# Inverse square roots of three mixers as powers on GpSimd, in a two-layer fp32 model on one core

## The chip, the cores and the metric

One core of a Trainium2 chip runs the whole program once. The metric is device time in microseconds (us), taken as the median of several runs. The engines are PE (TensorE, matmuls), DVE (VectorE), ACT (ScalarE), POOL (GpSimd) and SP (SyncE, which only issues DMAs here). Each takes its own instructions strictly in the order of its program and waits on counting semaphores for the others. Everything is float32.

## The reference, cut to what matters

Two blocks run one after the other on 256 tokens of width 1024. The first has two layers, each with three mixers side by side: HGRN2 (a gated linear recurrence), retention, and RWKV-7. The second has two layers of feed-forward, short convolution or latent attention, and attention to a memory; the change leaves its operations alone. The inverse square roots that the change touches are these:

```
# rwkv7_mixer, per head of 64
kk = kk * lax.rsqrt(jnp.sum(kk * kk, axis=-1, keepdims=True) + 1e-12)
y  = head_groupnorm(o, ln_g, ln_b, RWKV_GN_EPS) + bonus
# hgrn2_mixer
o  = rmsnorm(o.transpose(0, 2, 1, 3), norm_g)
# retention_mixer
o  = head_groupnorm(..., gn_g, gn_b, RET_GN_EPS)
# head_groupnorm
return (of - mu) * lax.rsqrt(var + eps) * g + b
```

## The kernel before

Each layer of the first block is cut into four quarters of the heads (q = 0 to 3). For each mixer and each engine there is a Python generator that issues that mixer's instructions for the four quarters and yields between steps: `rwkv_pe`, `rwkv_dve`, `rwkv_act`, `rwkv_pool` (called R), `hgrn_*` (H), `retention_*` (B, with no part on GpSimd). `weave` runs them by a string of `ORDER` that is written for each layer and engine: "R4 H2 B" means four steps of RWKV, two of HGRN, one of retention. So the order of instructions on each engine is fixed in the text, and an instruction that waits holds back all that stands behind it on its engine. After the mixers come the branch products (also woven), the output product, and then the second block, whose stages "conv", "queries" and "attention" have orders of their own.

On PE most steps of H and B, and the first sixteen of R in a quarter, are projections: 4 matmuls of the code with 256 columns, which the profile shows as 8 instructions (each fp32 matmul is two), from weights that SP loads into a ring of five slots. They need nothing but weights and a free PSUM bank, and so they are what fills PE's time while the recurrences, which are chains through PE, DVE, ACT and DMA, work out their next operand.

One quarter of RWKV goes like this. PE makes the projections, and from `rw_k` DVE forms `kk` and its square (L1100). PE sums the squares over each head with a matrix of ones (L787, "kkn"), which leaves the sum in every row, so the tile `rw_sig` with the sums is 128x512. DVE adds 1e-12 (L1103, "kkv"), ACT takes the root (L958, "kks"), DVE takes the reciprocal (L1108) and multiplies (L1110, "kk"). Only then may ACT overwrite `rw_sig` with the sigmoid of the decay code (L971), DVE scans it (L1130 to L1146), ACT takes exponentials (L976 to L980), DVE forms the operands (L1149 to L1158, "ops"), and PE makes the scores (L815 and L830). The rest of the quarter is a blockwise inverse on DVE (L660 to L701), which goes through DRAM and back, the products L729 to L895, and the same again for the backward direction; L848 is PE's first product with the masked scores.

At the end of a quarter each mixer norms its output `o`: DVE makes a variance of 4 or 8 numbers per partition ("varn", L1242 in `center_dve`, or L1524), ACT takes its root ("std": L1039 for RWKV, L1429 for HGRN, L1680 for retention), DVE the reciprocal (L1245 or L1527) and scales `o` (L1247 or L1529), and PE transposes it (L1289).

The HGRN loop has eight levels per quarter. For each, DVE (L1498, L1499) and POOL (L1563, L1564) form logarithms, ACT takes their exponentials (L1411, L1414), DVE (L1503) and POOL (L1568, L1570) multiply, PE makes the product (L1349) and DVE masks it in (L1511). POOL also sets `rw_scored_a` and `rw_scored_k` to zero twice in a quarter (L1061, L1062) and issues two small loads (L1054).

Of the kernel before, what the change touches and what calls it, by code (L numbers as in the profile page):

```python
# [10 lines left out]
ALU = mybir.AluOpType  # L11
# [100 lines left out]
def constants():  # L112
# [30 lines left out]
    for d, (strict, within) in enumerate(((p < c, p <= c), (p > c, p >= c))):  # L143
# [25 lines left out]
    ("conv", "tensor"):  # L169
        "C M2 C12 M2 C M2 C M C M C M C M C M C M C M C M2 C M C M C M C M3 C2 M C4 M C3 M3 C2 M3 C2 M21 ",  # L170
    ("queries", "tensor"):
        "Q M3 Q12 M3 Q2 M Q10 M2 Q M2 Q M4 Q M7 Q2 ",
    ("attention", "tensor"):
# [15 lines left out]
    ("conv", "vector"):  # L189
        "C M2 C10 M6 C4 M4 C5 M12 C M2 C2 M C M2 C M C M7 ",  # L190
    ("queries", "vector"):
        "Q M2 Q M Q6 M Q2 M3 Q7 M Q2 M Q M2 Q M Q M2 ",
    ("attention", "vector"):
# [3073 lines left out]
```

## Time and profile before

| | us |
|---|---|
| median of 3 runs | 3313.67 |
| lowest and highest | 3300.82 and 3321.72 |
| the profiled execution's own time | 3318.57 |
| its span, first to last instruction | 3316.7 |
| PE busy | 3075.4 |
| DVE busy | 1694.8 |
| ACT busy | 690.5 |
| POOL busy | 251.7 |

The profile is of one execution. Its own time is 1.9 us above its span and 4.9 us above the median, so a difference worked out in the trace is taken from 3318.57 and then moved down by 4.9. The two layers of mixers with their branches fill the first 2074 us of the span. The granted TensorE clock is given as a share of 2.4 GHz; the other level is 1.2 GHz, so a share c over a stretch means that 2(1-c) of it ran at 1.2 GHz.

### The profile page before, as it was taken

The numbers are of one execution on the slowest core, as the hardware profiler recorded it, in microseconds if no ns is written. First come the engines' busy times: TensorE is split into PE (matmuls) and PEld (weight loads), VectorE is DVE, ScalarE is ACT, GpSimd is POOL, SyncE is SP. The second block draws the span as 40 slices with busy tenths as digits, with TensorE's granted clock in tenths as the row PEclk, the third lists the DMA queues.
The fourth block names the chain that finished last, engine by engine and source line by source line (L and its number), as shares of the span: only waits on it lengthen the run. The fifth ranks groups of instructions, "written<-read, shape, count | busy, mean of one in ns | idle before, by whom it ended". The sixth has DMA issues, their size and how long they took to land. (4 is left out here: it accounts for less than half of the span.)

```text
span 3316.7 us, 45305 instructions
## 1 busy us (share of the span) xinstructions
PE 3075.4 (93%) x18996; PEld 2539.6 (77%) x18996; DVE 1694.8 (51%) x3491; ACT 690.5 (21%) x1343; POOL 251.7 (8%) x326
## 2 busy tenths in 40 slices
PE   8989997989999989999798999899979979997999
PEld 7878886868886878788687878695849749855794
DVE  3456556355321563755546421575237657746475
ACT  2323322132111232423123110100111011013100
POOL 0202121021000020202002100000000000000000
PEclk9999998989999999999798999999989989997999
DMA  5323232324324423333132243454425434531343
GB/s 206 104 79 125 78 114 79 102 70 130 117 93 156 151 66 107 103 92 118 41 123 77 76 142 140 148 170 159 152 78 173 169 111 141 174 108 76 127 167 126
DMA packets 153754, 395.56 MB, mean 119 GB/s; under 512 B 90288, under 2 KB 106800, under 8 KB 109648
## 3 DMA queue, kind: packets, MB, share of 16 engines
q1 hardware_dynamic: 51376, 367.94, 32.1%
q10 hardware_dynamic: 100608, 19.93, 3.0%
q0 software_dynamic: 1568, 4.79, 0.4%
q8 instruction: 151, 2.47, 0.3%
q14 instruction: 51, 0.42, 0.0%
HBM read 380.04 MB, written 12.59 MB: 118 GB/s over the span
## 5 line engine op out<-in xcount | busy, mean ns | idle before, releaser
L416 PE MATMUL bank<-h_features,weight_ring 128*128 128x256 f32 x4256 | 991.4, 389 | 7.8 <-DVE y_features L1266 2.8
L416 PEld LDWEIGHTS bank<-h_features,weight_ring 128*128 128x128 f32 x4256 | 812.2, 194 | 129.6 <-issue 7.3
L433 PE MATMUL bank<-weight_ring,h_features 128*128 128x256 f32 (+2 forms) x896 | 199.8, 375 | 2.0 <-DVE h_features L508 2.0
L433 PEld LDWEIGHTS bank<-weight_ring,h_features 128*128 128x128 f32 x896 | 162.5, 190 | 25.2 <-DVE h_features L508 2.3
L1922 PE MATMUL bank<-h_features,weight_ring 128*128 128x128 f32 x1408 | 171.9, 275 | 5.4 <-DVE h_features L508 5.4
L1922 PEld LDWEIGHTS bank<-h_features,weight_ring 128*128 128x128 f32 x1408 | 164.3, 192 | 6.1 <-DVE h_features L508 6.1
L1991 ACT COPY mem_normed<-bank 128x128 f32<-128x128 f32 x88 | 23.3, 265 | 482.6 <-PE bank L1922 476.9
L1746 PE MATMUL bank<-y_features,weight_ring 128*128 128x256 f32 x512 | 117.0, 380 | 0.0
L1746 PEld LDWEIGHTS bank<-y_features,weight_ring 128*128 128x128 f32 x512 | 95.9, 190 | 13.1 <-issue 0.7
L2074 DVE TENSOR_TENSOR mem_normed<-mem_normed,bank 128x256 f32<-128x256 f32 x88 | 37.1, 421 | 132.1 <-PE bank L1922 132.1
L1349 PE MATMUL bank<-hg_qs,hg_ks 128*128 128x128 f32 x512 | 76.2, 295 | 26.2 <-POOL hg_ks L1570 14.9
L1349 PEld LDWEIGHTS bank<-hg_qs,hg_ks 128*128 128x128 f32 x512 | 67.4, 202 | 37.3 <-DVE hg_qs L1503 25.0
L1922 PE MATMUL bank<-h_features,y_features 128*128 128x128 f32 x704 | 93.0, 275 | 0.0
L1922 PE MATMUL bank<-y_rwkv_features,y_hgrn_features 128*128 128x128 f32 x704 | 93.0, 275 | 0.0
L1922 PE MATMUL bank<-y_rwkv_features,y_features 128*128 128x128 f32 x704 | 93.0, 275 | 0.0
L1922 PE MATMUL bank<-ff_silu,weight_ring 128*128 128x128 f32 x704 | 93.0, 275 | 0.0
L1922 PE MATMUL bank<-h_features,y_hgrn_features 128*128 128x128 f32 x704 | 93.0, 275 | 0.0
L1922 PEld LDWEIGHTS bank<-h_features,y_features 128*128 128x128 f32 x704 | 85.7, 192 | 0.0
L1922 PEld LDWEIGHTS bank<-ff_silu,weight_ring 128*128 128x128 f32 x704 | 85.7, 192 | 0.0
L1922 PEld LDWEIGHTS bank<-y_rwkv_features,y_hgrn_features 128*128 128x128 f32 x704 | 85.7, 192 | 0.0
L1922 PEld LDWEIGHTS bank<-y_rwkv_features,y_features 128*128 128x128 f32 x704 | 85.7, 192 | 0.0
L1922 PEld LDWEIGHTS bank<-h_features,y_hgrn_features 128*128 128x128 f32 x704 | 85.7, 192 | 0.0
(520 smaller groups left out, 5003.7 us busy)
## 6 DMA issues: line engine op xcount, KB each, us to landing
weight_ring<-in_w_in SPq DMA_DIRECT2D x146, 1024.0 KB, 5.0
weight_ring<-in_f00w SPq DMA_DIRECT2D x33, 1024.0 KB, 4.8
weight_ring<-in_f01w SPq DMA_DIRECT2D x33, 1024.0 KB, 4.9
weight_ring<-in_f10w SPq DMA_DIRECT2D x33, 1024.0 KB, 4.8
weight_ring<-in_f11w SPq DMA_DIRECT2D x33, 1024.0 KB, 4.8
weight_ring<-in_w_b SPq DMA_DIRECT2D x16, 1024.0 KB, 4.8
weight_ring<-in_w_out SPq DMA_DIRECT2D x16, 1024.0 KB, 4.9
weight_ring<-in_conv_in SPq DMA_DIRECT2D x10, 1024.0 KB, 4.9
```

What stands on the lines that cost most here:

```text
L416: m = e.matmul(bank[:, j, :], w[:, k, j * P:(j + 1) * P], x[:, k, :], start=k == 0, stop=k == kt - 1, skip_group_check=True)
L433: m = e.matmul(bank[:, t * n:(t + 1) * n], x[:, k, t * P:(t + 1) * P], w[:, k, :], start=k == 0, stop=k == kt - 1, skip_group_check=True)
L1349: m = e.matmul(bank[:, t, h, :], H.k_[:, h, t * P:(t + 1) * P], H.q_[:, h, i * P:(i + 1) * P], start=True, stop=True, skip_group_check=True)
L1746: m = e.matmul(bank[:, j, :], w[:, k, j * P:(j + 1) * P], y[:, c * KT + k, :], start=k == 0 and c == 0 and j == 0, stop=k == KT - 1 and c ...
L1922: m = e.matmul(out, left[:, k, :], right[:, k, :], start=k == 0, stop=k == 3, skip_group_check=True)
L1991: e.copy(g.F.outs[at % 2][:, 7, :], g.banks.get(f, "p", c, 0)[:, 2 * P:3 * P]).then_inc(*S.act.up("first", f, c))
L2074: e.tensor_tensor(z[:, 0:2, :], z[:, 7:8, :].to_broadcast([P, 2, P]), first[:, 0:2, :], ALU.add).then_inc(*dve.up("u2", f, c))
```

## The change

The three roots on ACT and the reciprocals on DVE that follow them become one instruction on POOL each, a power with the exponent -0.5 from a one-column tile. The DVE steps that took the reciprocal now wait for POOL. Retention gets a generator on POOL for it. All the order strings are written anew, those of the second block too.

```diff
-        e.wait_ge(*dve.at("kkv", l, q))
-        e.activation(R.sig, R.sig, ACT.Sqrt).then_inc(*act.up("kks", l, q))
...
+def inverse_root_pool(e, g, S, z, *name):
+    e.tensor_tensor(z, z, g.minus_half.to_broadcast(list(z.shape)), ALU.pow).then_inc(*S.pool.up(*name))
...  rwkv_pool, in the loop over the quarters
         e.memset(R.state, 0.0).then_inc(*S.pool.up("state", l, q))
+        yield
+        e.wait_ge(*S.dve.at("kkv", l, q))
+        inverse_root_pool(e, g, S, flat(R.sig), "kks", l, q)
         for d in range(2):
...          the two memsets of scored_a and scored_k
+        yield
+        e.wait_ge(*S.dve.at("varn", l, q))
+        inverse_root_pool(e, g, S, R.var, "std", l, q)
...  rwkv_dve
-        e.wait_ge(*act.at("kks", l, q))
-        e.reciprocal(R.sig, R.sig).then_inc(*dve.up())
-        e.wait_ge(*dve.now())
+        e.wait_ge(*S.pool.at("kks", l, q))
         e.tensor_tensor(R.kk, R.kk, R.sig, ALU.mult).then_inc(*dve.up("kk", l, q))
...  center_dve, and in the same way hgrn_dve with H.ss
-    e.wait_ge(*S.act.at("std", *Q))
-    e.reciprocal(var, var).then_inc(*dve.up())
-    e.wait_ge(*dve.now())
+    e.wait_ge(*S.pool.at("std", *Q))
...  hgrn_pool, after the eight levels of a quarter
+        yield
+        e.wait_ge(*dve.at("varn", l, q))
+        inverse_root_pool(e, g, S, H.ss, "std", l, q)
...
+def retention_pool(e, g, l):
+    S, B = g.rt, g.B
+    for q in range(4):
+        yield
+        e.wait_ge(*S.dve.at("varn", l, q))
+        inverse_root_pool(e, g, S, B.var, "std", l, q)
+    yield
...  the start of two of the order strings
     ("mixers0", "tensor"):
-        "H2 R20 H2 R5 H11 R4 H R2 H6 B4 R2 B3 H B2 R B R5 H2 R2 B R B R H2 R2 B2 R4 B R4 H2 B R2 B R H2 R B R2 B "
+        "H2 R20 H2 R5 H7 R6 H11 R2 B5 R H R5 B R2 H2 R B R B2 R2 H2 R4 B R4 H2 B R2 B R H2 R B2 R2 B R6 H2 B4 H2 "
...
     ("mixers0", "gpsimd"):
-        "H R3 H10 R H6 R2 H16 R H10 R2 H6 R H9 R2 H7 R ",
+        "H B R4 H10 R H7 B R4 H16 R H B H4 R H R H2 R2 H8 B H2 R H5 R H R B H R2 H10 R2 ",
```

Read out step by step, the PE strings put this many projection steps (4 matmuls with 256 columns each) between the step with "kkn" and the first scores, L815, by quarter: layer 0: 11, 9, 4 and 10 before, 7, 8, 9 and 9 after; layer 1: 12, 9, 4 and 10 before, 10, 8, 4 and 9 after. The four steps with the code products stand there in both. In the DVE string of the first quarter of layer 0 two steps of H (L1451 to L1456) stand between L1133 and L1140 before, and none after. Between "kkv" and "kk" the DVE strings have no step of another mixer in the first quarter before or after; in the other quarters none to three, such as L1503.

In the POOL strings the power of "kks" stands right behind the loads and the memset of the state, before any HGRN level, in the first two quarters of layer 0 and the first of layer 1; in the second of layer 1 it stands behind the first level. In the third and fourth quarters it stands between the logarithms and the products of an HGRN level, or between two levels, and the power of RWKV's "std" of the quarter before stands one to three steps ahead of it, also inside the levels.

## Rows read from the trace of the kernel before

**Rows 1.** The page: busy time of each engine.
```profile
PE 3075.4 (93%) x18996; PEld 2539.6 (77%) x18996; DVE 1694.8 (51%) x3491; ACT 690.5 (21%) x1343; POOL 251.7 (8%) x326

```

**Rows 2.** Stretches: length, busy PE, PEld, DVE, ACT, POOL; granted clock, DMA share, GB/s.
```profile
0.00:2074.00 2074.00, 1915.42 (x12064) 1629.29 (x12064) 981.05 (x1927) 534.61 (x923) 248.69 (x320) 0.96 0.33 108
...
160.00:210.00 50.00, 37.19 (x213) 31.18 (x213) 42.81 (x79) 18.83 (x31) 11.25 (x13) 0.90 0.24 67
520.00:580.00 60.00, 38.29 (x167) 31.09 (x167) 49.01 (x88) 20.57 (x32) 9.16 (x12) 0.77 0.20 55
1560.00:1620.00 60.00, 40.15 (x167) 32.45 (x166) 48.45 (x87) 20.85 (x33) 9.16 (x12) 0.72 0.21 56
```

**Rows 3.** PE's waits up to 2120: for whom, us in total, times, longest.
```profile
PE bank L848 <- DVE rw_scored_k L1163: 31.2, 7, 6.7
...
PE bank L1349 <- POOL hg_ks L1570: 14.9, 5, 4.9
...
PE bank L815 <- DVE rw_a L1158: 7.4, 4, 2.0
```

**Rows 4.** The first quarter of layer 0 around "kks", in order of time.
```profile
61.12 0.68 DVE L1103 TENSOR_SCALAR rw_sig<-bank 128x512 f32<-128x512 f32 x1
...
65.89 0.69 DVE L1110 TENSOR_TENSOR rw_kk<-rw_kk,rw_sig 128x512 f32<-128x512 f32 x1
66.66 1.28 ACT L971 ACT_TABLE_LOAD   x1 [4.19 <-DVE rw_kk L1110]
...
72.84 0.17 DVE L1133 COPY rw_tot<-rw_bm 128x4 f32<-128x4 f32 x1
...
77.55 0.16 DVE L1140 TENSOR_SCALAR rw_mid<-rw_tot 128x4 f32<-128x4 f32 x1
...
82.46 0.69 DVE L1158 TENSOR_TENSOR rw_a<-rw_a,rw_bm 128x512 f32<-128x512 f32 x1
...
86.77 2.10 PE L815 MATMUL bank<-rw_kr,rw_a 64*128 64x256 f32 x16
```

**Rows 5.** From the chain that ended last: one projection step of PE.
```profile
2365.70 1.73 PE bank L416 x8
```

**Rows 6.** DVE's reciprocal of 128x512, and the two kinds of POOL product.
```profile
L1108 DVE RECIPROCAL rw_sig<-rw_sig 128x512 f32<-128x512 f32 x8 | 26.8, 3350 | 4.0 <-ACT rw_sig L958 4.0
...
L1568 POOL TENSOR_TENSOR hg_ks<-hg_ks,hg_kf 128x256 f32<-128x256 f32 x64 | 53.4, 835 | 177.5 <-ACT hg_ks L1414 177.5
L1563 POOL TENSOR_TENSOR hg_ks<-hg_bf 128x256 f32<-128x256 f32 x56 | 38.7, 691 | 301.2 <-PE bank L1349 301.2
```

**Rows 7.** The third quarter of layer 0 at "kks", in order of time.
```profile
525.05 1.00 DVE L1503 TENSOR_TENSOR hg_qs<-hg_qs,hg_q 128x512 f32<-128x512 f32 x1
...
525.47 1.18 POOL L1570 TENSOR_TENSOR hg_ks<-hg_ks,hg_kb 128x256 f32<-128x256 f32 x1
...
526.68 3.35 DVE L1108 RECIPROCAL rw_sig<-rw_sig 128x512 f32<-128x512 f32 x1 [0.62 <-ACT rw_sig L958]
...
530.07 0.69 DVE L1110 TENSOR_TENSOR rw_kk<-rw_kk,rw_sig 128x512 f32<-128x512 f32 x1
...
562.61 0.18 DVE L1245 RECIPROCAL rt_var<-rt_var 128x4 f32<-128x4 f32 x1 [2.79 <-ACT rt_var L1680]
```

**Rows 8.** PE at the end of the first quarter of layer 0.
```profile
202.57 1.11 PE L1289 MATMUL bank<-float_constants,hg_bf 128*128 128x128 f32 x4 [2.87 <-DVE hg_bf L1529]
```

**Rows 9.** ACT's table loads for the roots, by line.
```profile
L958 ACT ACT_TABLE_LOAD x8 | 10.3, 1283 | 0.1
...
L1429 ACT ACT_TABLE_LOAD x6 | 7.7, 1283 | 9.4 <-DVE rw_scored_k L1163 9.3
L1039 ACT ACT_TABLE_LOAD x6 | 7.7, 1283 | 0.1
...
L1680 ACT ACT_TABLE_LOAD x4 | 5.1, 1283 | 0.1
```

More of the change, by code:

```diff
@@ L149 @@
     ("mixers0", "tensor"):
[19 rows of a table removed]
[19 rows of a table added]
     ("conv", "tensor"):
-        "C M2 C12 M2 C M2 C M C M C M C M C M C M C M C M2 C M C M C M C M3 C2 M C4 M C3 M3 C2 M3 C2 M21 ",
+        "C M2 C12 M2 C M2 C M C M2 C M C M C3 M2 C M2 C M C2 M2 C2 M3 C2 M C4 M C3 M3 C2 M3 C M21 ",
     ("queries", "tensor"):
-        "Q M3 Q12 M3 Q2 M Q10 M2 Q M2 Q M4 Q M7 Q2 ",
+        "Q M3 Q12 M3 Q2 M Q6 M Q5 M3 Q M4 Q M7 Q2 ",
     ("attention", "tensor"):
[1 row of a table removed]
[1 row of a table added]
     ("mixers0", "vector"):
[13 rows of a table removed]
[15 rows of a table added]
     ("conv", "vector"):
-        "C M2 C10 M6 C4 M4 C5 M12 C M2 C2 M C M2 C M C M7 ",
+        "C M2 C10 M6 C4 M3 C5 M12 C M C M2 C2 M C M2 C M8 ",
     ("queries", "vector"):
-        "Q M2 Q M Q6 M Q2 M3 Q7 M Q2 M Q M2 Q M Q M2 ",
+        "Q M2 Q M Q6 M Q2 M3 Q6 M Q3 M Q M2 Q M Q M2 ",
     ("attention", "vector"):
[1 row of a table removed]
[1 row of a table added]
     ("mixers0", "scalar"):
[13 rows of a table removed]
[12 rows of a table added]
     ("conv", "scalar"):
@@ L213 @@
     ("attention", "scalar"):
-        "M X Y Z X M Y Z X2 M2 Y2 Z2 X M Y M2 Z X M X2 Y Z M2 X Y2 M Z2 M Y Z M X2 Y2 Z2 X M Y M2 Z X M X Y Z M2 "
-        "Y M Z M5 ",
+        "M X Y Z X M Y Z X2 M2 Z2 Y2 X M X M2 Y X2 Z M Y Z Y2 X M3 Z2 Y X2 M Z X M Y2 Z2 Y X M Z X Y M2 Y M Z2 M8 ",
     ("mixers0", "gpsimd"):
-        "H R3 H10 R H6 R2 H16 R H10 R2 H6 R H9 R2 H7 R ",
+        "H B R4 H10 R H7 B R4 H16 R H B H4 R H R H2 R2 H8 B H2 R H5 R H R B H R2 H10 R2 ",
     ("mixers1", "gpsimd"):
-        "R H R2 H10 R H6 R2 H16 R H10 R2 H6 R H9 R2 H7 R ",
+        "R H B R3 H12 R H5 B R2 H2 R2 H15 R B H7 R H R H R2 H7 B H R H5 R H R B H R2 H10 R2 ",
     ("mixers0", "sync"):
-        "H R4 H4 B6 H5 R4 B6 H5 B5 R4 B2 H2 B H B H B H B2 R4 B7 H4 B H B H B H B H B R8 ",
+        "H R4 H4 B6 H5 R4 B6 H5 B3 R4 B4 H2 B H B H B H B2 R4 B7 H3 B H B H2 B H B R7 H B R ",
     ("mixers1", "sync"):
-        "R4 H5 B6 H5 R4 B6 H5 B5 R4 B2 H2 B H B H B H B2 R4 B7 H4 B H B H B H B H B R8 ",
+        "R4 H5 B6 H5 R4 B6 H5 B5 R4 B2 H2 B H B H B H B2 R4 B7 H3 B H B H2 B2 H B R7 H R ",
     ("conv", "sync"):
@@ L955, in rwkv_act @@
             g.banks.empty(act, "vt", l, q, t)
-        yield
-        e.wait_ge(*dve.at("kkv", l, q))
-        e.activation(R.sig, R.sig, ACT.Sqrt).then_inc(*act.up("kks", l, q))
         for d in range(2):
@@ L1037, in rwkv_act @@
                     yield
-        e.wait_ge(*dve.at("varn", l, q))
-        e.activation(R.var, R.var, ACT.Sqrt).then_inc(*act.up("std", l, q))
-        yield
+def inverse_root_pool(e, g, S, z, *name):
+    e.tensor_tensor(z, z, g.minus_half.to_broadcast(list(z.shape)), ALU.pow).then_inc(*S.pool.up(*name))
 def rwkv_pool(e, g, l):
@@ L1427, in hgrn_act @@
         yield
-        e.wait_ge(*dve.at("varn", l, q))
-        e.activation(H.ss, H.ss, ACT.Sqrt).then_inc(*act.up("std", l, q))
-        yield
 def hgrn_dve(e, g, l):
@@ L1525, in hgrn_dve @@
         yield
-        e.wait_ge(*act.at("std", l, q))
-        e.reciprocal(H.ss, H.ss).then_inc(*dve.up())
-        e.wait_ge(*dve.now())
+        e.wait_ge(*S.pool.at("std", l, q))
         e.tensor_tensor(o3, o3, H.ss.unsqueeze(2).to_broadcast([P, 4, P]), ALU.mult).then_inc(
@@ L1678, in retention_act @@
             yield
-        e.wait_ge(*dve.at("varn", l, q))
-        e.activation(B.var, B.var, ACT.Sqrt).then_inc(*act.up("std", l, q))
-        yield
 def retention_dve(e, g, l):
@@ L3000, in clear_scratch_pool @@
     e.memset(g.nm_one, 1.0).then_inc(*g.st.pool.up("one"))
+    e.memset(g.minus_half, -0.5).then_inc(*g.st.pool.up())
     e.memset(zeros, 0.0).then_inc(*g.st.pool.up())
@@ L3011, in gpsimd_program @@
     for l in range(DEPTH):
-        weave(g, f"mixers{l}", "gpsimd", {"R": rwkv_pool(e, g, l), "H": hgrn_pool(e, g, l)})
+        weave(g, f"mixers{l}", "gpsimd", {"R": rwkv_pool(e, g, l), "H": hgrn_pool(e, g, l),
+                                          "B": retention_pool(e, g, l)})
     for S in (g.rw, g.hg, g.rt):
@@ L3075, in __init__ @@
         self.nm_ss, self.nm_one = sb("norm_sum", TT)[:, :], sb("norm_one", 1)[:, :]
+        self.minus_half = sb("minus_half", 1)[:, :]
         self.pos_i = sb("positions", TT, I32)[:, :]
```

87 rows, old and new, of the table ORDER are left out of this document.

## The prediction, made before the change was run

> **What bounds the kernel now.** I read the page's busy times first: PE is busy for 3075 us of 3317 and no other engine comes near it [rows 1]. So work that is taken from ACT or DVE is worth nothing by itself; it is worth what PE no longer waits. Next the stretches: the mixers take the first 2074 us, with PE busy for 1915, so 159 us are idle there. The idle time is not spread evenly. In 520 to 580, and in the same place of the next layer, 1560 to 1620, PE is busy for 38.3 and 40.2 of 60 us at a granted clock of 0.77 and 0.72, while DVE is busy for 49.0 and 48.5; 160 to 210 is the third such place [rows 2]. There DVE sets the pace. Then I read PE's waits by releaser: the largest, 31.2 us, is for the masked scores L1163 behind DVE's blockwise inverse, which the change doesn't touch; 14.9 us is for POOL's HGRN product; 7.4 us in four waits is for the operands L1158, whose chain begins at the root of "kks" [rows 3].
>
> **Part 1, the root of 128x512 ("kks"), 8 times.** Now: the sum with 1e-12 ends at 61.12 + 0.68 = 61.80 and the multiplication L1110 starts at 65.89, so root, reciprocal and hand-overs take 4.1 us; behind L1110 ACT loads a table for 1.28 us before the sigmoid L971 [rows 4]. The new order has one POOL instruction there, X us long. No row shows a power on POOL. From below: POOL's product L1563, 691 ns for 256 numbers per partition, or L1568, 835 ns, gives 1.4 to 1.7 us for 512 [rows 6]. From above: DVE's iterative RECIPROCAL of 512 takes 3.35 us [rows 6]; POOL's product takes 1.67 us for 512 against 0.69 for DVE's L1110 [rows 4, 6], so a function like the reciprocal at POOL's rate would be 3.35 x 2.4 = 8 us, and a power made of a logarithm, a product and an exponential as some ten passes over the data, each like a product of POOL, 15 us or more. I take 1.7 us, because the instruction is POOL's TENSOR_TENSOR with another operation and the rows nearest to it are POOL's TENSOR_TENSOR rows; the range keeps 1.4 to 15. The step is then 4.1 - 1.7 = 2.4 us shorter, and 1.3 us more where the sigmoid's table is still in, which it now can be, for no root comes between: 3.7 us of chain, 8 times.
>
> How long may X be before PE waits? In the first quarter the operands are ready at 82.46 + 0.69 = 83.15, and PE comes to L815 at 86.77 [rows 4]. The new string takes 4 of the 11 projection steps away from between; a step is 1.73 us [rows 5], so PE comes at about 79.9, or some 3 us earlier if its clock is full. The operands come earlier by 4.1 - X, by the table's 1.3 and by the 4.5 us between L1133 and L1140 (72.84 + 0.17 to 77.55), where H stood and doesn't now [rows 4]: at 73.3 + X. So X has room up to 3.5 to 6.5 us here; I take 5 for all quarters. Over both layers the strings take 5 projection steps net (8.7 us) out of this gap and put them in front of other waits.
>
> What PE gets back, by place:
> - 520 to 580, twice: DVE is the pace. L1503 came straight behind L1103 at 525.05, so L1110 could start at 525.05 + 1.7 = 526.8 in place of 530.07: 3.2 us. The root of retention makes DVE wait 2.79 us at 562.61, and a power of 4 numbers with its hand-over takes perhaps 0.3: 2.5 us [rows 7]. Together 5.7, twice: 11.4 us. A part of the 1.2 GHz time goes with it: 2 x 0.23 x 60 = 28 us of the first of these stretches ran at 1.2 GHz [rows 2], where busy PE loses half. I take 3 us for both.
> - The end of the first quarter, twice: PE waits 2.87 us for HGRN's normed output at 202.57 [rows 8]. The step is shorter by a table load of 1.28 us, and the new PE string has five steps of B in front of it: 2 x 2.9 = 5.7 us.
> - Two of the four waits of L815 for L1158 [rows 3] follow a "kks": 3.5 us.
> - The 5 steps set free, in front of the waits of L848 and L1349: of 8.7 us I count 3, since the planner of the order can't place them everywhere.
> Sum: 11.4 + 3 + 5.7 + 3.5 + 3 = 27 us.
>
> **Part 2, the 24 small roots.** Eight for each mixer, of 4 or 8 numbers per partition. A root, a reciprocal (0.18 us at 562.61) and where needed a table load of 1.28 us go; a POOL instruction on so few numbers comes. The gains on PE's path are in the list above. The rest is hidden: 8 + 6 + 6 + 4 = 24 loads for roots, 30.8 us of ACT [rows 9], on an engine that is busy for a fifth of the span. DVE loses 26.8 us of long reciprocals and some 4 us of short ones out of 981 in the mixers [rows 2, 6].
>
> **Part 3, POOL's queue.** POOL's own time is free (249 us busy of 2074 [rows 2]). But POOL now waits inside its order for "varn" and "kkv", and behind that stand the next HGRN logarithms and products, for which PE waits already (14.9 us in 5 waits [rows 3]). In third and fourth quarters such a wait stands between the logarithms and the product of a level. In the first quarter only the memsets of the scores stand behind it, due more than 10 us later. I count nothing for this in the forecast, and price it below.
>
> **Part 4, the other strings** (conv, queries, attention) move a few steps and no work; nothing, within 3 us either way.
>
> **A shared path between DVE and POOL.** L1503, a DVE product with both operands in SBUF, took 1.00 us at 525.05 while POOL ran, and POOL's L1570, which then overlapped it, took 1.18 us at 525.47 [rows 7] against 0.69 for DVE's product of the same shape L1110 and 835 ns for POOL's products [rows 4, 6]. One held the other up. The Trainium skill, page "SBUF — State Buffer", section "SBUF: two separate sides", says that the shared ports of the two are locked for a whole instruction and that a DVE operation with two SBUF inputs then waits it out; the trace agrees, with these two rows. By that rule a long power would also hold the L1503 that some new DVE strings put between "kkv" and "kk", but L1110 waits behind it anyway: it adds one product, 0.7 us, in those quarters.
>
> **The rivals.**
> Rival 1, the power is slow. It decides from X = 5 us on: DVE stands at L1110 and every other mixer's DVE step behind it too, so each further us is one us of PE in each of 8 quarters, and a quarter more for the lower clock. The gain of 27 is used up at X = 5 + 27/10 = 7.7 us. At X = 12 the price is 7 x 8 x 1.25 = 70 us, of the gain about 20 stay: +50, so 3369 by the profiled execution's count and 3364 as a median. For it: a power is no simple operation, and even DVE takes 6.5 ns per number for a reciprocal, five times its product. Against it: the fastest rows of that kind on POOL. The Trainium skill, page "GPSIMD Engine Reference", section "Elementwise — side-by-side cycle accounting", says that bodies of three or more operations run at roughly 3 operations a cycle at 1.2 GHz; if a power were 40 operations, an estimate by that page is 13.3 x 512 / 1.2 GHz = 5.7 us, and with 80 operations 11 us. No row here shows it.
> Rival 2, POOL's queue eats the gain. Four waits a layer (the "kkv" and RWKV's "varn" in the inner quarters) stand inside HGRN levels; if each holds PE's L1349 by 2.5 us, half of the longest such wait now (4.9 [rows 3]), that is 20 us: -7 in all, 3311 by the profiled count, 3307 as a median.
> Rival 3, it doesn't do what it says: ACT goes on loading tables, because exponential, sigmoid and logarithm alternate, so the 1.28 us behind L1110 stays. That costs 8 x 1.3 = 10 us of chain and at most 5 us of PE: inside rival 2's range.
>
> **How the numbers follow.** The forecast: 3318.6 - 27 = 3291.6 by the profiled execution's count, 4.9 lower as a median: 3287. Chance 0.48, its own range 3262 to 3305. Rivals 2 and 3 with no measurable change, a power between 5 and 9 us among them: 0.24, 3300 to 3325. Rival 1: 0.28, from 3340 up; at X = 15 the price is 10 x 8 x 1.25 = 100, less 20: 3394. The range leaves out the upper half of rival 1 and a little below: 3258 to 3375. One per cent is 33 us, about what a measurement of this kernel can tell from no change. The forecast passes that bound in 4 cases of 10, 0.20 in all; rival 1 gives 0.28 slower; the rest, 0.52, is within one per cent.
>
> **What would show it.** In the profile after: one POOL TENSOR_TENSOR on `rw_sig` x8; near 1.7 us the forecast holds, over 5 rival 1. L1110 starts some 2 us behind the end of L1103. No table loads for roots in the mixers, and ACT's loads fewer by 24 or more. DVE's wait at 562 gone, PE busier than 38 us in what was 520 to 580. Rival 2 would show as more than 15 us of waits of L1349 for POOL, with POOL idle before its powers. What would make all of it wrong: the new order leaving PE without projections at a place that was full before.

## The result, and the profile after

The changed kernel takes 3942.64 us (median of 4 runs, 3934.4 to 3948.25) against 3317.69 us for the kernel before in the same session: a ratio of 1.1905, 95% interval 1.187 to 1.1939. It is 625 us slower. The forecast was 3287 us with a range up to 3375, so it was wrong by far, and outside the range.

First the page of the kernel after: the span, the busy time of each engine, and in the slices the rows of PE, POOL and PE's granted clock.

```profile
span 3940.1 us, 45238 instructions
...
PE 3087.7 (78%) x18996; PEld 2547.8 (65%) x18996; DVE 1662.1 (42%) x3459; ACT 633.8 (16%) x1275; POOL 946.7 (24%) x359
...
PE   6497489288199947856963973998998998998899
...
POOL 4523612811910063164156037000000000000000
PEclk9698799689699978977986996999998999998799
```

PE does the same work as before, 3087.7 us against 3075.4 [rows 1], in a span 623.4 us longer: it stands idle for 852 us where it was idle for 241. POOL is busy for 695 us more. In the slices PE is at 2 and 1 tenths where POOL is at 8 and 9, and at 3 to 6 where POOL is at 4 to 7, where a power is split over two slices. The chain that ended last, by engine, and the groups of the new instruction (the name of the group, then busy us and mean ns, then the idle time of POOL ahead of it):

```profile
PE 66%; POOL 17%; DVE 10%; DMA 4%; issue 1%; ACT 1%; ACTq 0%; DVEq 0%; SPq 0%
...
L1037 POOL TENSOR_TENSOR rw_sig<-rw_sig,minus_half 128x512 f32<-128x512 f32 x8 | 657.5, 82187 | 233.8 <-DVE rw_sig L1106 233.7
```

One power of 512 numbers per partition takes 82.2 us. The forecast took 1.7 us, from the rows of POOL's products [rows 6]. The small ones, from the groups of POOL:

```profile
L1037 POOL TENSOR_TENSOR rw_var<-rw_var,minus_half 128x8 f32<-128x8 f32 x8 | 14.6, 1827 | 275.2 <-DVE rw_var L1243 275.2
...
L1037 POOL TENSOR_TENSOR hg_ss<-hg_ss,minus_half 128x4 f32<-128x4 f32 x8 | 8.4, 1056 | 106.5 <-DVE hg_ss L1520 106.5
```

(1827 - 1056) / 4 = 193 ns for each number by these two, (82187 - 1827) / 504 = 159 ns from 8 to 512. So the small powers of this kernel alone would have said some 99 us for 512 numbers (193 ns x 512, an estimate).

Who waits for it. PE's waits (for whom, us in total, times, longest), which answer to [rows 3]:

```profile
PE bank L1348 <- POOL hg_ks L1564: 394.4, 8, 78.8
PE bank L815 <- DVE rw_a L1159: 85.9, 5, 78.4
PE bank L1333 <- DVE hg_ks L1477: 80.2, 1, 80.2
PE bank L416 <- DVE hg_q L1437: 78.6, 1, 78.6
PE bank L848 <- DVE rw_scored_k L1164: 38.8, 11, 7.1
```

The first two were 14.9 and 7.4 us before, and the third and fourth had no row; they grew by 394.4 - 14.9 + 85.9 - 7.4 + 80.2 + 78.6 = 617 us. PE's idle time as a whole grew by 611 us and its busy time by 12, so these four are the loss. Eight of these waits are 77 to 80 us long, one for each power. And seven of the eight are not for anything that the power makes. In five PE waits at L1348 for POOL's HGRN product L1564, which stands behind the power on POOL; in two it waits for HGRN steps of DVE (L1477, L1437), which stand behind L1111 on DVE. Only the one at L815 is for the key norm's own chain. The third quarter of layer 0, in order of time over POOL, DVE and PE (start, length):

```profile
672.10 0.61 POOL L1558 TENSOR_TENSOR hg_ks<-hg_bb 128x256 f32<-128x256 f32 x1
...
674.07 0.69 DVE L1106 TENSOR_SCALAR rw_sig<-bank 128x512 f32<-128x512 f32 x1 [0.75 <-PE bank L787]
...
674.85 82.34 POOL L1037 TENSOR_TENSOR rw_sig<-rw_sig,minus_half 128x512 f32<-128x512 f32 x1 [2.13 <-DVE rw_sig L1106]
...
757.22 0.69 DVE L1111 TENSOR_TENSOR rw_kk<-rw_kk,rw_sig 128x512 f32<-128x512 f32 x1 [81.86 <-POOL rw_sig L1037]
...
759.81 0.72 POOL L1562 TENSOR_TENSOR hg_ks<-hg_ks,hg_kf 128x256 f32<-128x256 f32 x1
```
```profile
761.37 2.05 PE L1348 MATMUL bank<-hg_qs,hg_ks 128*128 128x128 f32 x8 [78.31 <-POOL hg_ks L1564]
```

The power stands on POOL's queue between the logarithms of an HGRN level (L1557, L1558) and its products (L1562, L1564). DVE waits for the power for 81.86 us, and PE for the product behind it for 78.31. The stretch of the first power, 62 to 144, by engine (columns as in [rows 2]), and the same in two parts:

```profile
62.00:144.00 82.00, 12.68 (x58) 10.56 (x56) 0.42 (x1) 0.00 (x0) 82.00 (x2) 0.61 0.18 73
...
62.00:80.00 18.00, 12.68 (x58) 10.56 (x56) 0.00 (x0) 0.00 (x0) 18.00 (x1) 1.00 0.80 332
80.00:144.00 64.00, 0.00 (x0) 0.00 (x0) 0.42 (x1) 0.00 (x0) 64.00 (x2) 0.50 0.00 0
```

PE is busy for 12.7 of 82 us, DVE for 0.4, ACT not at all. PE's work ends at 76.8, still at 2.4 GHz (granted clock 1.00); from 80 on PE does nothing and the granted clock is 0.50, that is 1.2 GHz.

### The profile page after: what moved, and what is told of

Read it like the earlier page. It is cut to its first block, busy times and chain, and to the rows that moved or that the text cites. A ratio compares the mean times of both kernels' runs of the same rounds, so it can differ in the third digit from the quotient of the medians.

```text
span 3940.1 us, 45238 instructions
## 1 busy us (share of the span) xinstructions
PE 3087.7 (78%) x18996; PEld 2547.8 (65%) x18996; DVE 1662.1 (42%) x3459; ACT 633.8 (16%) x1275; POOL 946.7 (24%) x359
## 4 chain that ended last, share of the span: by engine, by line
PE 66%; POOL 17%; DVE 10%; DMA 4%; issue 1%; ACT 1%; ACTq 0%; DVEq 0%; SPq 0%
PE bank L416 20%; POOL rw_sig L1037 17%; PE bank L1925 14%; PE bank L1943 5%; PE bank L1749 4%; PE bank L1812 3%; PE bank L433 3%; PE bank L1348 1%; DMA rw_ex<-xT_scratch 1%; DVE rw_ex L660 1%; PE bank L1954 1%; DMA rw_sig<-scores_scratch 1%; PE bank L729 1%; PE bank L748 1%; PE bank L830 1%
## 5 line engine op out<-in xcount | busy, mean ns | idle before, releaser
L416 PE MATMUL bank<-h_features,weight_ring 128*128 128x256 f32 x4256 | 988.9, 388 | 88.0 <-DVE hg_q L1437 78.6
L1037 POOL TENSOR_TENSOR rw_sig<-rw_sig,minus_half 128x512 f32<-128x512 f32 x8 | 657.5, 82187 | 233.8 <-DVE rw_sig L1106 233.7
L1348 PE MATMUL bank<-hg_qs,hg_ks 128*128 128x128 f32 x512 | 81.5, 309 | 402.3 <-POOL hg_ks L1564 394.4
L1348 PEld LDWEIGHTS bank<-hg_qs,hg_ks 128*128 128x128 f32 x512 | 72.1, 215 | 411.9 <-issue 401.4
L1111 DVE TENSOR_TENSOR rw_kk<-rw_kk,rw_sig 128x512 f32<-128x512 f32 x8 | 5.5, 692 | 651.5 <-POOL rw_sig L1037 651.5
L815 PE MATMUL bank<-rw_kr,rw_a 64*128 64x256 f32 x256 | 36.8, 425 | 85.9 <-DVE rw_a L1159 85.9
L1557 POOL TENSOR_TENSOR hg_ks<-hg_bf 128x256 f32<-128x256 f32 x56 | 36.4, 650 | 277.6 <-PE bank L1348 277.6
L1562 POOL TENSOR_TENSOR hg_ks<-hg_ks,hg_kf 128x256 f32<-128x256 f32 x64 | 54.8, 856 | 183.6 <-ACT hg_ks L1413 183.4
L1557 POOL TENSOR_TENSOR hg_ks<-hg_totf,hg_bf 128x256 f32<-128x256 f32 x8 | 5.7, 716 | 375.7 <-PE bank L1333 375.7
```

The source lines that it names most:

```text
L416: m = e.matmul(bank[:, j, :], w[:, k, j * P:(j + 1) * P], x[:, k, :], start=k == 0, stop=k == kt - 1, skip_group_check=True)
L1037: e.tensor_tensor(z, z, g.minus_half.to_broadcast(list(z.shape)), ALU.pow).then_inc(*S.pool.up(*name))
L1348: m = e.matmul(bank[:, t, h, :], H.k_[:, h, t * P:(t + 1) * P], H.q_[:, h, i * P:(i + 1) * P], start=True, stop=True, skip_group_check=True)
L1557: e.tensor_tensor(level_first(H.k_, level), rf, level_first(H.bf, level), ALU.subtract).then_inc(*pool.up())
L1562: e.tensor_tensor(level_first(H.k_, level), level_first(H.k_, level), level_first(H.kf, level), ALU.mult).then_inc(*pool.up())
```

## The experiments

The question was first whether the length of the power is the whole loss, or whether the new strings or the small powers carry a part; then why the instruction is slow; then who has to wait for it; and last what was left of the forecast once the power is short. "Orders" and "strings" mean the same, the texts that fix each engine's sequence; "new" are those of the changed kernel, "old" those of the kernel before. All ratios are to the kernel before in the same session, with 95% intervals.

**Fewer numbers in the power, new orders.** Three kernels with 16, 64 and 256 of the 512 numbers:

```
-        inverse_root_pool(e, g, S, flat(R.sig), "kks", l, q)
+        inverse_root_pool(e, g, S, R.sig[:, :, 0:8], "kks", l, q)      # 0:32, 0:128
-        e.tensor_tensor(R.kk, R.kk, R.sig, ALU.mult)
+        kk4 = R.kk.rearrange("p n (a s) -> p n a s", s=8)              # 32, 128
+        e.tensor_tensor(kk4, kk4, R.sig[:, :, 0:8].unsqueeze(2).to_broadcast([P, 2, T // 8, 8]), ALU.mult)
```

> The changed kernel with the key norm's power on 16 of the 512 numbers of a partition; the product that follows takes those 16 repeated, so most tokens are normed with another token's sum. All else, the new orders included, as in the changed kernel. The power should last about 2.9 us (16 x 0.16 + 0.4) in place of 82.2. Theory A, the length of the power is all of the loss: with a power that fits the room of some 5 us the time falls back to the forecast's neighbourhood, 3280 to 3330 us. Theory B, the new orders or the small powers carry a part of the loss: 3400 us or more stay. Theory C, a wait for GpSimd as such (its queue, its hand-over) costs: 3340 to 3400 us.

> As the run with 16 numbers, with 64 of 512: a power of about 10.6 us. Theory A: each us beyond a room of some 5 us costs one us in each of 8 quarters, so 8 x 5.6 = 45 us above the run with 16 numbers, 3330 to 3380 us; by the forecast's slope of 10 us for each us of power it is 56 above. If the room were nothing, 62 above the 16 numbers. Theory B: 3450 us or more, and little difference from the run with 16 numbers.

> As the runs with 16 and 64 numbers, with 256: a power of about 41.3 us. Between 64 numbers (3378 us) and 512 (3943 us) the time rose 7.9 us for each us of power; on that line it is 3378 + 30.7 x 7.9 = 3620 us. Were there another room further out (work of the other mixers that could cover 30 us), the time would lie well below the line, under 3560 us; with the clock falling only in the longest waits it would lie below it as well.

Measured: 16 numbers 3302.9 us (0.996, 0.9938 to 0.9981); 64 numbers 3378.3 us (1.0167, 1.0124 to 1.0209); 256 numbers 3622.75 us (1.0934, 1.0878 to 1.099). The groups of the power in the three:

```profile
L1038 POOL TENSOR_TENSOR rw_sig<-rw_sig,minus_half 128x16 f32<-128x16 f32 x8 | 25.2, 3155 | 233.2 <-DVE rw_sig L1107 233.1
```
```profile
L1038 POOL TENSOR_TENSOR rw_sig<-rw_sig,minus_half 128x64 f32<-128x64 f32 x8 | 86.3, 10784 | 232.9 <-DVE rw_sig L1107 232.8
```
```profile
L1038 POOL TENSOR_TENSOR rw_sig<-rw_sig,minus_half 128x256 f32<-128x256 f32 x8 | 331.1, 41386 | 234.6 <-DVE rw_sig L1107 234.5
```

Theory A holds: the time follows the length, and 3620 was expected for the third. Theories B and C fall: with a short power nothing of the loss is left. The slope is (3622.75 - 3378.3) / (41.4 - 10.8) = 8.0 us for each us of power, and (3942.6 - 3622.75) / (82.2 - 41.4) = 7.8 beyond: one us of PE in each of 8 quarters, with nothing on top. From 16 to 64 numbers it is 75.4 / 7.6 = 9.9, although the first of these microseconds still fall into the room. Here PE's busy time rises, from 3065.3 to 3094.9 us, and then no more (3089.4 with 256 numbers, 3087.7 with 512). In the kernel with an addition, below, it is 3074.3, so the rise is 13 to 30 us. That it is the lower clock after the waits fits a row of the full kernel: the scores L815 behind the first long wait take 3.75 us, the ones at 242.86 take 2.07. PE's waits with 64 numbers show the order that the full power has:

```profile
PE bank L1351 <- POOL hg_ks L1567: 39.4, 8, 7.5
...
PE bank L815 <- DVE rw_a L1162: 13.2, 5, 5.3
```

The room is the length of a power that PE's other work covers. By the longest waits it is 10.8 - 7.5 = 3.3 us where the HGRN product stands behind the power, and in the full kernel 82.2 - 78.8 = 3.4. In the first quarter PE waits at L815 for the operands. These are the rows of it with 64 numbers:

```profile
61.04 10.56 POOL L1038 TENSOR_TENSOR rw_sig<-rw_sig,minus_half 128x64 f32<-128x64 f32 x1 [44.07 <-DVE rw_sig L1107]
...
83.29 3.92 PE L815 MATMUL bank<-rw_kr,rw_a 64*128 64x256 f32 x16 [5.26 <-DVE rw_a L1162]
```

10.6 - 5.3 = 5.3 us of room there, what the forecast had taken for all quarters. With the full power that place has 82.0 - 78.4 = 3.6.

**An addition in place of the long power, new orders.** The same instruction form, operands, waits and place; only the operation differs.

```
+    op = ALU.add if name[0] == "kks" else ALU.pow
-    e.tensor_tensor(z, z, g.minus_half.to_broadcast(list(z.shape)), ALU.pow)
+    e.tensor_tensor(z, z, g.minus_half.to_broadcast(list(z.shape)), op)
-        e.tensor_scalar(R.sig, pairs(g.banks.get("kkn", l, q)), 1.0, 1e-12, ALU.mult, ALU.add)
+        e.tensor_scalar(R.sig, pairs(g.banks.get("kkn", l, q)), 1e-6, 0.501, ALU.mult, ALU.add)
```

> The changed kernel with an addition in place of the key norm's power: the same instruction form on all 512 numbers (a tensor and a broadcast column, on GpSimd), the same waits and orders; VectorE scales the sum so that what comes out is small. It leaves out the key norm. If GpSimd does a power like a product, as the forecast had it, the addition would last as long as the power (82 us) and the time stay at 3940; if it is the operation that is slow, the addition lasts 1.4 to 1.9 us, what the rows of products gave the forecast for the power, and the time is what the forecast's own mechanism gives once its length holds: 3287 us by the sum, 3295 to 3305 us by the run with 16 numbers (3303 with a power of some 2.9 us).

Measured: 3303.6 us (0.9968, 0.9948 to 0.9987). The group of the addition:

```profile
L1038 POOL TENSOR_TENSOR rw_sig<-rw_sig,minus_half 128x512 f32<-128x512 f32 x8 | 10.2, 1272 | 234.3 <-DVE rw_sig L1107 234.2
```

So neither the shape, nor the broadcast operand, nor the engine is slow; the power is, 65 times the addition (82.2 / 1.27). This run also is the forecast's own case, a POOL instruction under 1.7 us in that place: it gives -14.5 us (-17 to -4 by the interval) where the sum had -27. The run with 16 numbers lies at the same time with a power 1.9 us longer, so between 1.3 and 3.2 us the length doesn't show in the time, although PE's waits at L815 are 13.4 us there and 7.5 here.

**The price of a power by itself.** Single operations of 128 numbers per partition on a tile of their own, behind the mixers.

```
+    e.tensor_tensor(z, z, half.to_broadcast([P, 128]), ALU.pow)                      # L3029, z = 3.7
+    e.tensor_tensor(z, z, w, ALU.pow)                                                # L3031, w = -0.5
+    e.tensor_tensor(z[0:64], z[0:64], half[0:64].to_broadcast([64, 128]), ALU.pow)   # L3033
+    e.tensor_tensor(z[0:16], z[0:16], half[0:16].to_broadcast([16, 128]), ALU.pow)   # L3035
+    e.tensor_tensor(z, z, half.to_broadcast([P, 128]), ALU.mult)                     # L3037
+    e.tensor_tensor(z, z, half.to_broadcast([P, 128]), ALU.pow)                      # L3041, z = 1.0
+    e.tensor_tensor(z, z, w, ALU.pow)                                                # L3046, 3.0 to the 2.0
```

> The kernel before with the 24 small powers on GpSimd, and behind the mixers, while GpSimd has nothing to do, a row of single operations of 128 numbers per partition on a tile of their own: the power with a broadcast exponent, with the exponent as a full tensor, on 64 and on 16 partitions, with all numbers 1.0, 3.0 to the 2.0, and a product. Theory: about 0.16 us for each number of a partition, so 20 to 21 us each whatever the partitions, the values and the exponent's form, and 0.3 to 0.6 us for the product. Rival 1, partitions are worked off in turns: 64 partitions take half. Rival 2, the broadcast column is what is slow: the full tensor is far faster. Rival 3, the length hangs on the values: 1.0 to a power, or an exponent of 2, is faster.

Measured, POOL's groups in that kernel (the kernel's time, 3311.2 us in one run, plays no part):

```profile
L3033 POOL TENSOR_TENSOR price<-price,minus_half 64x128 f32<-64x128 f32 x1 | 21.1, 21143 | 0.1
L3046 POOL TENSOR_TENSOR price<-price 128x128 f32<-128x128 f32 x1 | 20.9, 20932 | 0.1
L3041 POOL TENSOR_TENSOR price<-price,minus_half 128x128 f32<-128x128 f32 x1 | 20.9, 20904 | 0.1
L3031 POOL TENSOR_TENSOR price<-price 128x128 f32<-128x128 f32 x1 | 20.8, 20771 | 0.1
L3029 POOL TENSOR_TENSOR price<-price,minus_half 128x128 f32<-128x128 f32 x1 | 20.8, 20761 | 0.1
L3035 POOL TENSOR_TENSOR price<-price,minus_half 16x128 f32<-16x128 f32 x1 | 20.7, 20705 | 0.1
L3037 POOL TENSOR_TENSOR price<-price,minus_half 128x128 f32<-128x128 f32 x1 | 0.5, 477 | 0.1
```

All six powers take 20.7 to 21.1 us, 162 ns for each number of a partition; the product takes 0.48. All three rivals fall: the partitions run side by side, the exponent's form and the values tried make no difference.

**The same power, read by nobody.** The long power stays on POOL's queue where it was, behind the same wait, but works on a tile of its own; DVE multiplies by the scaled sum and waits for no power.

```
-        inverse_root_pool(e, g, S, flat(R.sig), "kks", l, q)
+        inverse_root_pool(e, g, S, g.aside, "kks", l, q)
-        e.tensor_scalar(R.sig, pairs(g.banks.get("kkn", l, q)), 1.0, 1e-12, ALU.mult, ALU.add)
+        e.tensor_scalar(R.sig, pairs(g.banks.get("kkn", l, q)), 1e-6, 1e-3, ALU.mult, ALU.add)
-        e.wait_ge(*S.pool.at("kks", l, q))
+        e.wait_ge(*dve.now())
```

> The changed kernel with the eight long powers kept on GpSimd's queue, at the same point and behind the same wait, but made on a tile of their own that nobody reads; VectorE multiplies by the scaled sum as it came from the bank and waits for no power. It leaves out the key norm. So VectorE's wait is gone and GpSimd's queue is blocked as before. In the changed kernel's trace the tensor engine's long waits are five for HGRN's products behind the power on GpSimd's queue and three for steps behind VectorE's wait. Theory Q, the queue alone is enough: the five stay, and the products and memsets behind the power in the other three quarters come late as well, 3303 + 5 x 79 = 3700 us at least, up to 3940. Theory V, what counts is VectorE's wait and the queue's lateness only follows from it: 3300 to 3400 us.

Measured: 3899.3 us (1.1773, 1.1709 to 1.1836). Against the addition in the same place that is 596 us, 93% of the 639 that the full power costs, though no engine reads its result. PE's waits there:

```profile
PE bank L1348 <- POOL hg_ks L1564: 393.4, 8, 78.9
PE bank L830 <- DVE rw_scored_a L1164: 197.7, 5, 65.9
```

The five long waits for HGRN's product are as long as in the changed kernel, 393.4 us against 394.4 (in 8 waits each). In the other three quarters PE now waits for the masked scores, for which DVE waited in turn for the cleared tile:

```profile
DVE rw_scored_a L1164 <- POOL rw_scored_k L1062: 205.5, 3, 69.4
```

L1062 is POOL's memset, which is queued behind the power as well. Theory Q holds: the blocked queue is enough. The three waits at L830 are 65.3 to 65.9 us where the changed kernel has 78.4 to 80.2 in these quarters, which is 40 of the 43 us that went. So a kernel that left this queue as it is and only used the result later could have gained no more than some 43 us. The opposite isn't shown: no run has DVE wait 82 us with POOL's queue open. In these three quarters DVE's wait held PE first, so the two causes overlap, and the 93% is what the queue does alone, not what would go if only the queue were freed.

**New orders and small powers, old key norm.** The changed kernel with the root on ACT (in the step of the first low-rank projection) and the reciprocal on DVE:

```
+                        e.wait_ge(*dve.at("kkv", l, q))
+                        e.activation(R.sig, R.sig, ACT.Sqrt).then_inc(*act.up("kks", l, q))
                         e.wait_ge(*dve.at("kk", l, q))
...
-        e.wait_ge(*S.pool.at("kks", l, q))
+        e.wait_ge(*act.at("kks", l, q))
+        e.reciprocal(R.sig, R.sig).then_inc(*dve.up())
+        e.wait_ge(*dve.now())
```

> The changed kernel's orders and its 24 small powers on GpSimd, but the key norm's root back on ScalarE (in the step of the first low-rank projection) and its reciprocal back on VectorE. Theory A: 3290 to 3340 us, within 1.5% of the kernel before. Theory B (orders or small powers): 3400 us or more.

Measured: 3331.1 us (1.0045, 1.0023 to 1.0067).

**Old orders and small powers, old key norm.** The kernel before with the 24 small roots moved; only POOL's strings are new.

```
-        e.wait_ge(*dve.at("varn", l, q))
-        e.activation(R.var, R.var, ACT.Sqrt).then_inc(*act.up("std", l, q))
...
+        yield
+        e.wait_ge(*S.dve.at("varn", l, q))
+        inverse_root_pool(e, g, S, R.var, "std", l, q)
```

> The kernel before with its own orders and the key norm as it was; only the 24 small roots are powers on GpSimd, placed on its queue where the roots stood in time. The powers last 1.0 and 1.8 us against 3.3 us of table load, root, hand-over and reciprocal now, and none of them is on the tensor engine's path for long. Theory A: 3290 to 3325 us, no measurable difference. Theory C (any wait for GpSimd's queue costs): above 3340 us. Between this run and the one with the new orders the difference is what the new orders do.

Measured: 3308.6 us (0.9977, 0.9953 to 1.0001). As expected no difference that can be told from nothing. ACT's busy time falls from 690.5 to 653.2 us (26 table loads of 1.28 us fewer make 33 of it) and DVE's from 1694.8 to 1691.1, and PE doesn't feel it. With the run above it says what the new strings do to the old key norm: 3331.1 - 3308.6 = 22.5 us slower. That run's place of the root on ACT was my choice, and it has a price: from the start of the sum to the start of the product DVE's step takes 6.1 to 6.3 us in each of its eight quarters (49.2 us together), because the table load now comes behind the sum, while in the old orders it takes 4.8 to 6.6 (43.6 together). So a part of the 22.5 belongs to that and not to the strings.

**Old orders, a short power.** The run above, and the key norm as a power on 16 numbers, placed on POOL's queue where the root stood in time; the edit of the power is that of the first experiment.

> The kernel before's own orders with all powers on GpSimd, the key norm's on 16 of 512 numbers (the product takes them repeated, so most tokens are normed with another token's sum); its step on GpSimd's queue stands where the root stood in time. A power of 3.2 us in place of a table load, a root and a reciprocal. With the new orders the same edit was worth 28 us (3303 against 3331), which is the forecast's sum of 27, but the new orders with the old key norm lay 22 us above the old orders (3331 against 3309). Theory A, the gain of a short chain and the cost of the new orders are separate: 3309 - 28 = 3275 to 3290 us here. Theory B, the new orders are fitted to a short key norm, and the old ones to the long one (with them the tensor engine has other work there): no gain here, 3300 to 3315 us.

Measured: 3309.0 us (0.9979, 0.9962 to 0.9997), the same as without this edit. Theory B's time came. In the third quarter of this kernel:

```profile
524.04 0.69 DVE L1111 TENSOR_SCALAR rw_sig<-bank 128x512 f32<-128x512 f32 x1 [0.93 <-PE bank L787]
...
526.20 2.93 POOL L1041 TENSOR_TENSOR rw_sig<-rw_sig,minus_half 128x16 f32<-128x16 f32 x1
...
529.16 0.69 DVE L1117 TENSOR_TENSOR rw_kk<-rw_kk,rw_sig 128x512 f32<-128x512 f32 x1 [3.51 <-POOL rw_sig L1041]
```

The sum is ready at 524.73 and POOL starts at 526.20, for it was still busy with other work, so the step takes 529.16 - 524.04 = 5.1 us where root and reciprocal took 5.6 in the kernel without this edit. The third quarters gain least: in the other six the step takes 3.7 us where it took 4.8 or 6.6, and over all eight 32.6 us where it took 43.6. So the step is 11 us shorter in all, and the time doesn't show it.

**Old orders, the key norm as exp(-0.5 ln x) on ACT.** An attempt at a better kernel: no reciprocal, no POOL.

```
-        e.activation(R.sig, R.sig, ACT.Sqrt).then_inc(*act.up("kks", l, q))
+        e.activation(R.sig, R.sig, ACT.Ln).then_inc(*act.up())
+        e.wait_ge(*act.now())
+        e.activation(R.sig, R.sig, ACT.Exp, scale=-0.5).then_inc(*act.up("kks", l, q))
```

> The kernel before with the 24 small powers on GpSimd; the key norm as exp(-0.5 ln x), both on ScalarE, so that VectorE's reciprocal of 3.35 us goes and ScalarE gets one more pass of some 0.6 us. On the chain between the bank and the product 1.5 to 2.8 us less, or nothing less if each of the two passes loads a table (2 x 1.28 us). Theory A (the tensor engine waits here for the length of this chain): by the run with 16 numbers, 10 to 25 us less than the run without this edit (3309), 3285 to 3300 us. Rival, the table loads eat it: 3305 to 3325 us.

Measured: 3312.25 us (0.998, 0.9955 to 1.0005), no difference. The third quarter of it, around the two passes:

```profile
522.84 0.69 DVE L1110 TENSOR_SCALAR rw_sig<-bank 128x512 f32<-128x512 f32 x1 [0.93 <-PE bank L787]
...
523.11 1.28 ACT L958 ACT_TABLE_LOAD   x1
...
525.06 1.28 ACT L960 ACT_TABLE_LOAD   x1
...
527.01 0.69 DVE L1115 TENSOR_TENSOR rw_kk<-rw_kk,rw_sig 128x512 f32<-128x512 f32 x1 [2.57 <-ACT rw_sig L960]
```

Each pass loads a table, and the time is the rival's. But the loads don't eat the gain of the step: it is 5.6 - (527.01 - 522.84) = 1.4 us shorter at this place and 15.3 us shorter over the eight quarters (28.3 against 43.6). This, too, is worth nothing in the old orders.

No complete version beats the kernel before by more than these runs can tell. The fastest that computes the reference, old orders with small powers, lies 9 us below it and its interval takes in a ratio of 1. The runs with 16 numbers and with the addition bound what a short key norm could bring in these strings: 0.4% and 0.3%. Each head's sums stand in all 64 partitions of the head, so a layout with the tokens on the partitions would need 8 numbers for each in place of 512, by the small powers' row an estimated 1.8 us; it takes transposes on PE at both ends, and wasn't tried.

## Why the prediction was wrong, step by step

- **What bounds the kernel.** Right: work taken from ACT and DVE is worth nothing by itself. DVE lost 33 us and ACT 57, and the small powers moved the time by 9 us at most.
- **X = 1.7 us, "because the instruction is POOL's TENSOR_TENSOR with another operation".** This step failed. It alone took the time out of the range: with an instruction of 1.3 or 3.2 us in its place the same kernel takes 3303 to 3304 us. The form says nothing about the operation: 1.27 us for the addition, 82.2 for the power. The bound from above was wrong as well: ten passes like a product gave 15 us, and the power is as long as 65 additions of the same shape. The forecast ranked two unlike rows by their name; the nearer kin of a power was DVE's iterative reciprocal [rows 6], and even at POOL's rate that gave a tenth.
- **The room.** 5 us were taken for all quarters, from the first. By the longest waits it is 3.3 to 3.4 where the HGRN product is queued behind the power, in the first quarter 5.3 with 64 numbers and 3.6 with 512, and in the second of layer 0 with 512 only 82.0 - 80.2 = 1.8.
- **Rival 1, its mechanism and its price.** Right in kind: a power longer than the room costs one us of PE for each us in each of 8 quarters, and the runs give 7.8 to 8.0. The quarter more for the clock was wrong over the long stretch: PE's busy time rises by 13 to 30 us once, when the waits come, and by nothing for each further us. While it waits PE has no work that could run slowly (0.00 us busy from 80 to 144, at 0.50). By the rival's own line, with 20 of the gain left, a power of 82.2 us gives 3313.7 - 20 + 77.2 x 10 = 4066; 3943 came. The chance of 0.28 stood on this rival, but the lengths that it priced, 12 and 15 us, were less than a fifth of the one that came.
- **Where the wait sits.** Rival 1 put it at DVE's L1110 (now L1111). DVE does wait there, 651.5 us in all, but the run with the unread power shows that 93% of the loss stays when it doesn't. Whether DVE's wait alone would cost as much was not tried.
- **Part 3, POOL's queue: "I count nothing".** The text named the very place, a wait between the logarithms and the product of a level, and asked only what it costs to wait for "kkv". What it didn't ask is how long the queue is shut by the instruction itself. Of the memsets it said that they are due more than 10 us later; behind 82 us they too were late, and PE waited 65.9 us at L830 in the run with the unread power. With a short power it was right to count nothing: PE's wait for POOL's HGRN product fell from 14.9 us to 3.8 in the run with the addition, so rival 2 falls too:

```profile
PE bank L1349 <- POOL hg_ks L1565: 3.8, 4, 2.3
```

- **The gains by place, 27 us.** Mis-sized, and this is told apart from X by the addition: -14.5 us. At two of its places the gain came. The two waits of 2.87 us for `hg_bf` at the end of the first quarters [rows 8] are gone, and in the stretches that answer to 520 to 580 and 1560 to 1620 (513.3 to 573.3 and 1550.6 to 1610.6) PE is busy for 46.4 and 42.2 us where it was for 38.3 and 40.2. L815 brought nothing (7.4 us in waits, now 7.5). What the sum lacks is a term for new waits that the new strings make elsewhere. These are of the kernel with the addition, at the end of the second and the third quarter of layer 0, and both are in the run with the old key norm in the new strings as well (6.62 and 9.14 us):

```profile
383.95 1.11 PE L1289 MATMUL bank<-float_constants,hg_bf 128*128 128x128 f32 x4 [6.63 <-DVE hg_bf L1524]
...
717.55 1.11 PE L1289 MATMUL bank<-float_constants,rw_o 128*128 128x128 f32 x4 [9.14 <-DVE rw_o L1247]
...
PE bank L1289 <- DVE rw_o L1247: 13.6, 4, 9.1
```

In the kernel before PE waits for `rw_o` in no row. The forecast's last sentence comes near to this, the new order leaving PE without projections at a place that was full before, but no term of the sum stood for it.

- **New strings and short step belong together.** The forecast treated the step's 3.7 us as a gain that any order could take. A short step is worth 28 us in the new strings (3331.1 to 3302.9, the step 17.5 us shorter over the eight quarters) and nothing in the old ones (3308.6 to 3309.0, the step 11.0 us shorter), while the new strings cost 22.5 with the long step. Both 28 and 22.5 hold the price of the root's place in the run with the old key norm in the new strings, so they are upper bounds. That the old strings put other work where PE would have waited is my reading; [rows 4] fit it, with the operands ready 3.6 us before PE comes to L815, but no run separates it. What the net of 14.5 us is made of, place by place, stays open.
- **Part 2 and rival 3.** The table loads went from 146 to 110 in all, 36 fewer where 24 or more were foreseen, so rival 3 falls. The small powers take 1.04 to 1.06 us on 4 numbers and 1.83 on 8. DVE waits 0.26 to 2.73 us for those of retention (mean of seven waits 1.15), at the forecast's two places 0.57 and 1.12 where it had 2.79 before; 0.3 was taken.
- **The shared path between DVE and POOL.** The forecast expected a DVE product with two SBUF operands to wait out a long power. It doesn't; at most it is held by 0.8 us at the power's start. See the last section.

## What to carry to other kernels

An instruction that no row shows has no price, and its form (engine, opcode, shape) gives none: measure it once by itself, at two sizes, before an order is built on it; here the two small sizes of the changed kernel would have said 193 ns a number, near enough to the 160 of the long one. Ask of a slow instruction not only who reads its result but what is queued behind it on its own engine: here the blocked queue alone makes 93% of the loss. And a step that is made shorter in an order written out in full is worth what that order left uncovered, which may be nothing.

## What the runs showed of the hardware

**A power on GpSimd (float32) costs some 160 ns for each number of a partition**: about 1.05 us for 4, 1.83 for 8, 3.16 for 16, 10.8 for 64, 20.8 for 128, 41.4 for 256 and 82.2 for 512. At 128 numbers it is the same on 16, 64 and 128 partitions, for the exponents -0.5 and 2 and for a column or a full tensor as exponent. An addition of 128x512 in the same form takes 1.27 us. The Trainium skill, page "GPSIMD Engine Reference", section "Elementwise — side-by-side cycle accounting", counts a long body at roughly 3 operations a cycle of 1.2 GHz; an estimate by that page from the 162 ns of the single powers is some 580 operations for each number, where the forecast had tried 40 and 80.

**The long power doesn't hold up DVE for its length.** In the kernel with the unread power, the second quarter of layer 0, POOL's power and DVE's products beside it:

```profile
349.09 81.95 POOL L1037 TENSOR_TENSOR aside<-aside,minus_half 128x512 f32<-128x512 f32 x1 [28.41 <-DVE rw_sig L1106]
```
```profile
363.30 0.69 DVE L1150 TENSOR_TENSOR rw_kr<-rw_kk,rw_sig 128x512 f32<-128x512 f32 x1
...
365.83 0.69 DVE L1159 TENSOR_TENSOR rw_a<-rw_a,rw_bm 128x512 f32<-128x512 f32 x1
```

L1150 and L1159 read two operands from SBUF in the midst of a POOL instruction that reads SBUF too, and take 0.69 us, what such a product takes with POOL idle [rows 4]. Only at the start of a power is there a hold: in four of the eight quarters DVE's L1111 starts 0.44 us into the power and takes 1.53 us in place of 0.69, as here in the third:

```profile
651.15 82.34 POOL L1037 TENSOR_TENSOR aside<-aside,minus_half 128x512 f32<-128x512 f32 x1 [2.13 <-DVE rw_sig L1106]
651.59 1.53 DVE L1111 TENSOR_TENSOR rw_kk<-rw_kk,rw_sig 128x512 f32<-128x512 f32 x1
```

The only other single row of DVE's in the eight powers that is over 0.15 us longer than its kind is a scan of 1.15 us for 0.68, and it starts 0.42 us into the power of the second quarter. In that kernel DVE is busy for 1661.7 us in all, in the one with 16 numbers for 1661.6, though POOL's powers run for 633 us more. The Trainium skill, page "SBUF — State Buffer", section "SBUF: two separate sides", has the shared ports locked for a whole instruction, with the other engine fully blocked. The trace doesn't agree for this one: the longest hold is 0.84 us of 82. The short conflicts of [rows 7], 1.00 us for a DVE product beside a POOL product, do exist. One reading is that the hold goes with the accesses and not with the instruction; no run here tests it.

**TensorE's granted clock fell once it had no work.** It is 1.00 from 62 to 80 us of the changed kernel, with PE busy for 12.7 of 18 us, and 0.50 from 80 to 144, with PE busy for none. The scores L815 that follow take 3.75 us where the next ones take 2.07.
